# Modulation pieces of a two-layer diffusion trunk: placed in another order at the start, in attention and in the last norm gap, and a state term of the scan placed earlier

## What is computed

```python
sc, scc = jax.nn.silu(c), jax.nn.silu(c_ctx)
for l in range(DEPTH):
    m_lat = sc @ w_mod[l] + b_mod[l]          # 9 x 1024 values for the latent tokens
    m_ctx = scc @ w_mod[l] + b_mod[l]         # and for the context tokens
    h = half_ffn(h, shift0, scale0, gate0, ...)      # norm, modulate, SwiGLU, norm, gate
    u = modulate(h, g[2], shift1, scale1)
    y = token_mixing(u, ...)                  # MLA, windowed attention, gated DeltaNet, Mamba-2
    h = h + gate1 * rms_norm(y @ w_out, g[3])
    h = half_ffn(h, shift2, scale2, gate2, ...)

def modulate(x, g_pre, shift, scale):
    return rms_norm(x, g_pre) * (1.0 + scale) + shift
...
o = decay * (q @ S) + within-chunk part       # DeltaNet: S is the state, carried over 4 chunks
```

## Time and profile before

| | |
|---|---|
| median of 3 runs | 2270.41 us (2266.66 to 2270.74) |
| the profiled execution | 2268.9 us, its span 2267.0 us |
| mean granted TensorE clock | 0.961 of full |
| TensorE matmul busy | 2116.7 us, 93% |
| VectorE, ScalarE, GpSimd busy | 1088.5, 804.9, 213.8 us |
| read from HBM | 255.97 MB |

### The profile page before, as it was taken

The page is one execution under the profiler, slowest core; times in us unless marked ns, Lnnn a source line. Parts: engine busy times, 40 slices in busy tenths (PEclk is TensorE's granted clock), DMA queues, the critical chain, the costliest instruction groups (busy, mean ns, idle before and its releaser), DMA issues.

```text
span 2267.0 us, 31510 instructions
## 1 busy us (share of the span) xinstructions
PE 2116.7 (93%) x13261; PEld 1740.9 (77%) x13261; DVE 1088.5 (48%) x1598; ACT 804.9 (36%) x1277; POOL 213.8 (9%) x312
## 2 busy tenths in 40 slices
PE   6999999899989988999999899999989987888997
PEld 4778888687845876888888688888869765778997
DVE  4323233576284476433334633333464547576555
ACT  3322223354345433321232422122344434334443
POOL 0000000100013441000000200000020022420000
PEclk8999999999999999999999899999968999998999
DMA  9464352423235514323423342432332312434662
GB/s 286 129 194 114 118 131 77 151 75 98 67 102 186 186 57 130 93 70 107 112 76 101 112 112 64 121 104 70 108 121 65 119 38 94 131 103 121 177 169 83
DMA packets 403325, 259.07 MB, mean 114 GB/s; under 512 B 21850, under 2 KB 401904, under 8 KB 403184
## 3 DMA queue, kind: packets, MB, share of 16 engines
q1 hardware_dynamic: 403184, 257.06, 38.9%
HBM read 255.97 MB, written 1.05 MB: 113 GB/s over the span
## 4 chain that ended last, share of the span: by engine, by line
PE 81%; DVE 11%; ACT 4%; issue 2%; SPq 1%; DMA 0%; POOL 0%; POOLq 0%; DVEq 0%; ACTq 0%
PE bank L827 23%; PE bank L828 22%; PE bank L829 22%; PE bank L750 2%; PE bank L732 1%; DVE uT L2048 1%; DVE wl L1984 1%; PE bank L1174 1%; PE bank L1077 1%; ACT wh L1488 1%; DVE uT L2046 1%; PE bank L1106 1%; PE bank L779 1%; PE bank L771 1%; SPq L568 1%
## 5 line engine op out<-in xcount | busy, mean ns | idle before, releaser
L827 PE MATMUL bank<-uh,wh 128*128 128x512 f32 (+1 forms) x1504 | 549.6, 365 | 22.8 <-DVE ul L2054 15.5
L828 PE MATMUL bank<-ul,wh 128*128 128x512 f32 (+1 forms) x1504 | 546.3, 363 | 0.0
L829 PE MATMUL bank<-uh,wl 128*128 128x512 f32 (+1 forms) x1504 | 546.2, 363 | 0.0
L1984 DVE TENSOR_TENSOR wl<-ring,wh 128x2048 fp32r<-128x2048 f32 (+1 forms) x155 | 312.5, 2016 | 161.2 <-ACT wh L1488 160.4
L1488 ACT ACTIVATE wh<-ring 128x2048 fp32r<-128x2048 f32 (+1 forms) x158 | 267.2, 1691 | 302.9 <-PE bank L829 293.5
L827 PEld LDWEIGHTS bank<-uh,wh 128*128 128x128 f32 x1504 | 286.7, 191 | 72.0 <-issue 17.2
L829 PEld LDWEIGHTS bank<-uh,wl 128*128 128x128 f32 x1504 | 286.4, 190 | 43.8
L828 PEld LDWEIGHTS bank<-ul,wh 128*128 128x128 f32 x1504 | 286.8, 191 | 42.7
L827 PE MATMUL bank<-hh,wh 128*128 128x512 f32 (+1 forms) x704 | 255.5, 363 | 1.4 <-DVE wl L1984 1.4
L828 PE MATMUL bank<-hl,wh 128*128 128x512 f32 (+1 forms) x704 | 255.2, 363 | 0.0
L829 PE MATMUL bank<-hh,wl 128*128 128x512 f32 (+1 forms) x704 | 255.2, 362 | 0.0
(11 more groups left out here) (321 smaller groups left out, 2772.4 us busy)
## 6 DMA issues: line engine op xcount, KB each, us to landing
ring<-in_ffn_w_dram SPq DMA_DIRECT2D x176, 512.0 KB, 5.2
ring<-in_w_mod_dram SPq DMA_DIRECT2D x136, 512.0 KB, 4.6
ring<-in_ffn_w_dram SPq DMA_DIRECT2D x64, 384.0 KB, 3.6
...
```

Source lines behind the costliest of these rows:

```text
L827: pe.matmul(bank, w_hi, x_hi, start=first, stop=False)
L828: pe.matmul(bank, w_hi, x_lo, start=False, stop=False)
L829: return pe.matmul(bank, w_lo, x_hi, start=False, stop=last)
L1984: TT(low[:, b, 0:floats], at, high[:, b, 0:floats].bitcast(F32), ALU.subtract).then_inc(wl_ready, 1)
```

## The change

At the start, two modulation pieces are loaded ahead of the first weight piece and six behind it; the eight are taken in pairs of one shift and one scale piece (`START_COLUMN`), each pair gives the gains of two feature blocks (`start_gains`), and the last two pairs are multiplied between the products of the first weight piece (`first_piece`). In attention the turn of a modulation row stands behind the scores of the next pair, and the column copy behind that pair's second exponential. Three pieces of layer 1's attention are moved to its middle gap. In the last scan step `add_state` stands ahead of `split_out`.

```diff
--- before.py
+++ after.py
@@ -118,13 +118,13 @@
-    MOD_PLAN = {("start", 0): RING, ("spare", 0): 4, ("ffn0", 0): 9, ("ffn1", 0): 3, ("gap0", 0): 3, ("mix", 0): 27, ("gap1", 0): 3,
-                ("gap2", 0): 3, ("gap0", 1): 3, ("mix", 1): 13}
+    MOD_PLAN = {("start", 0): 2, ("start1", 0): 1, ("spare", 0): 5, ("ffn0", 0): 9, ("ffn1", 0): 3, ("gap0", 0): 3, ("mix", 0): 27, ("gap1", 0): 3,
+                ("gap2", 0): 3, ("gap0", 1): 3, ("mix", 1): 10, ("gap1", 1): 3}
     assert sum(MOD_PLAN.values()) == LAYERS * MOD_PIECES
     MOD_AFTER = {("up0", 0, 0): ("ffn0", 0), ("up1", 0, 0): ("ffn1", 0)}
-    GAP_BEFORE = {("in", 0): ("gap0", 0), ("up0", 0, 1): ("gap1", 0), ("up0", 1, 0): ("gap2", 0),
-                  ("in", 1): ("gap0", 1)}
+    GAP_BEFORE = {("up0", 0, 0): ("start1", 0), ("in", 0): ("gap0", 0), ("up0", 0, 1): ("gap1", 0), ("up0", 1, 0): ("gap2", 0),
+                  ("in", 1): ("gap0", 1), ("up0", 1, 1): ("gap1", 1)}
     for l in range(LAYERS):
@@ -319,11 +319,17 @@
         crow = view(29696, P)
-        spare = view(8192, 4, 2048)
+        spare = [view(at, 2048) for at in (20480, 22528, 24576, 10240, 14336)]
         uTf = uT[:, :, :].rearrange("p k t -> p (k t)")
         HEAD_DMAS, MOD_PARAM_DMAS, PARAM_DMAS = 4, LAYERS * 2, 2 + LAYERS * 15
-        START_MODS = MOD_PLAN["start", 0] + MOD_PLAN["spare", 0]
+        START_COLUMN = (0, 4, 1, 5, 2, 6, 3, 7)
+        def column_of(g):
+            l, p = divmod(g, MOD_PIECES)
+            return l, START_COLUMN[g] if g < KC else p
         NORM_AT = (195, 195, 193, 194)
@@ -505,7 +511,7 @@
-        MIX_PIECES = ((15, 8, 4, 0), (5, 4, 4, 0))
+        MIX_PIECES = ((15, 8, 4, 0), (2, 4, 4, 0))
@@ -571,7 +577,7 @@
             def mod_piece(g):
-                l, p = divmod(g, MOD_PIECES)
+                l, p = column_of(g)
                 n = MOD_PIECE[g]
@@ -595,6 +601,14 @@
                 return srcs
+            def spare_mods():
+                for i in range(MOD_PLAN["spare", 0]):
+                    l, p = column_of(MOD_FIRST["spare", 0] + i)
+                    src = rows(w_mod[l])[:, :, p * 256:(p + 1) * 256]
+                    dst = spare[i].rearrange("p (k w) -> p k w", k=KC)
+                    for h in (0, 4):
+                        sp.dma_start(dst[:, h:h + 4, :], src[:, h:h + 4, :]).then_inc(sem(f"spare_landed{i}"), 16)
@@ -603,6 +617,8 @@
                             mod_pieces(GAP_BEFORE.get((f"up{part}", l, f)))
+                        if (l, f, part, j) == (0, 0, 0, 0):
+                            spare_mods()
                         if ffn_mod(l, f, part, j) is not None:
@@ -624,13 +640,6 @@
                     sp.dma_start(dst, src).then_inc(sem("mod_params_in"), 16)
-            for i in range(MOD_PLAN["spare", 0]):
-                g = MOD_FIRST["spare", 0] + i
-                src = rows(w_mod[0])[:, :, g * 256:(g + 1) * 256]
-                dst = spare[:, i, :].rearrange("p (k w) -> p k w", k=KC)
-                for h in (0, 4):
-                    sp.dma_start(dst[:, h:h + 4, :], src[:, h:h + 4, :]).then_inc(sem(f"spare_landed{i}"), 16)
             def params(i):
@@ -739,7 +748,7 @@
                     pe.wait_ge(sem(f"spare_landed{i}"), 32)
-                    weights = spare[:, i, :]
+                    weights = spare[i]
                 else:
@@ -828,6 +837,23 @@
+            def first_piece():
+                def blocks(first, last):
+                    for k in range(first, last):
+                        wait_low(pe, 0, 0, k)
+                        for g in range(2):
+                            ws = slice((g * KC + k) * P, (g * KC + k + 1) * P)
+                            done = split_product(ps[g][:, :], (wh[:, 0, ws], wl[:, 0, ws]), (uh[:, k, :], ul[:, k, :]),
+                                                 k == 0, k == KC - 1)
+                            if k == KC - 1:
+                                done.then_inc((w1_done, pieces_done)[g], 1)
+                mod_work(4, 6, banks=(6, 7))
+                blocks(0, 2)
+                mod_work(6, 8, banks=(6, 7))
+                blocks(2, 8)
             def ffn(l, f, hs):
@@ -840,6 +866,9 @@
                         pe.wait_ge(gated, g0 + j - 1 + GATE_CREDIT)
+                        if (l, f, part, j) == (0, 0, 0, 0):
+                            first_piece()
+                            continue
                         fresh = part == 0 and j == 0
@@ -1114,13 +1143,13 @@
                 for p in range(pairs + 2):
-                    if p and att_mod(l, p - 1) is not None:
-                        mod_turn(att_mod(l, p - 1), ps[7])
                     if p < pairs:
                         biases(2 * p + 1)
+                    if p and att_mod(l, p - 1) is not None:
+                        mod_turn(att_mod(l, p - 1), ps[7])
                     if p >= 2:
@@ -1409,14 +1438,13 @@
             pe.wait_ge(cond_ready, 1)
-            mod_work(0, 4, banks=(0, 1))
+            mod_work(0, 2, banks=(0, 1))
             start_sums()
             setup_params(0, ps[2])
-            mod_work(4, 6, banks=(0, 1))
             spread(0, ps[PRE_BANK], (0, 1))
-            mod_work(6, START_MODS, banks=(0, 1))
-            pe.wait_ge(mod_copied, START_MODS)
+            mod_work(2, 4, banks=(6, 7))
+            pe.wait_ge(mod_copied, 4)
             for l in range(LAYERS):
@@ -1542,6 +1570,8 @@
                 for m in range(KC):
+                    if p == 0 and m in (2, 6):
+                        mod_work(*{2: (4, 6), 6: (6, 8)}[m], banks=(6, 7))
                     if 0 in hs:
@@ -1761,10 +1791,10 @@
                         exp(2 * p)
+                    if p < pairs:
+                        exp(2 * p + 1)
                     if p and att_mod(l, p - 1) is not None:
                         mod_column_out(att_mod(l, p - 1), ps[7])
-                    if p < pairs:
-                        exp(2 * p + 1)
                     if p:
@@ -1923,12 +1953,11 @@
             load_sqrt()
-            mod_work(0, 4, banks=(0, 1))
+            mod_work(0, 2, banks=(0, 1))
+            round_piece(PIECES["up0", 0, 0][0], 2048)
+            norm(0, ps[PRE_BANK], (0, 1))
             setup_mod_params()
-            norm(0, ps[PRE_BANK], (0, 1))
-            mod_work(4, 6, banks=(0, 1))
-            mod_work(6, START_MODS, banks=(0, 1))
-            round_piece(PIECES["up0", 0, 0][0], 2048)
+            mod_work(2, 4, banks=(6, 7))
             prenorm_blocks(0, 0)
@@ -2010,6 +2039,18 @@
+            def start_gains(i):
+                dve.wait_ge(mod_copied, 2 * i + 2)
+                at = slice(2 * i, 2 * i + 2)
+                both = modT[:, 0, 0:2 * KC, :].rearrange("p (s m) v -> p s m v", s=2)[:, :, at, :]
+                bias = prm[:, 0, 0:2 * KC].rearrange("p (s m) -> p s m", s=2)[:, :, at]
+                link(TT(both, both, wide(bias, 2), ALU.add))
+                link(STT(gpre[:, 0, at], modT[:, 0, KC + 2 * i:KC + 2 * i + 2, :], 1.0,
+                         wide(prm[:, 0, 72 + 2 * i:74 + 2 * i], 2), ALU.add, ALU.mult))
+                if i == 0:
+                    V.memset(small[:, 58:59], 0.0).then_inc(mod_ready, 1)
             def post_gains(l, j):
@@ -2043,6 +2084,8 @@
                             wait_x(dve, p - 1, m)
+                        elif m % 2 == 0:
+                            start_gains(m // 2)
                         TT(u[:, m, t0:T], xT[:, m, t0:T], ps[PRE_BANK][:, t0:T], ALU.mult).then_inc(x_scaled, 1)
@@ -2497,12 +2540,14 @@
                             finish_inverses(l, 0).then_inc(sem("first_inverses"), 1)
+                        add_state(n, ts, [gate(2, d, 0) for d in range(2)])
                         if early_out(l):
                     if outputs:
-                        add_state(n, ts, [gate(2, d, 0) for d in range(2)])
+                        if n < NT - 1:
+                            add_state(n, ts, [gate(2, d, 0) for d in range(2)])
                         dve.wait_ge(sem("og_ready"), f + 1)
@@ -2619,9 +2664,8 @@
             norm(0, (0, 1))
+            split_rest(PIECES["up0", 0, 0][0], 2048)
             dve.wait_ge(sem("params_act"), 1)
-            pre_gains(0, 0)
-            split_rest(PIECES["up0", 0, 0][0], 2048)
             prenorm_blocks(0, 0)
```

## The result

The changed kernel takes 2257.52 us in the median of five runs (2256.56 to 2260.51). The ratio to the kernel before is 0.995, with a 95% interval of 0.9935 to 0.9964: 8 to 15 us less. Run again beside others it took 2258.02 us, ratio 0.9946 (0.9928 to 0.9965). The forecast was 2256.5. The profiled execution is the slowest of its five, 2260.51 us, so that its span is only 8.3 us under the one of the earlier trace rows.

A forecast was written before the change was run, and what follows sets the result against it. TensorE was taken as the bound (81% of the chain, VectorE 11%), with gains only where it waits. Terms -7.0 - 6.2 - 0.3 - 1.8 + 2.2 = -13.1 gave 2256.5 us, range 2248 to 2263.

The forecast's parts named there:

- The start, -7.0: Start: with loads reordered, the second weight piece begins at 53.4 to 55.0, not 61.34; 7.0 us gained, ends 2.3 and 9.8.
- Ready at 53.2: Start: the second weight piece's low part, 8.0 us from the scaling of block 6 at about 45.2, is ready at 53.2.
- Layer 0's attention, -6.2: Layer 0's attention: 15 waits for a modulation row, 8.5 us, mostly vanish; 6.2 us gained, ends 8.5 and 2.0.
- nothing is lost there, little is left to lose: Layer 0's attention: column copy behind the second exponential comes 2.6 us later, as TensorE reaches the product; no loss.
- the lower end: Layer 0's attention: gain of only 2.0 us if release by the second exponential takes back 0.3 a pair.
- the slower rival: Attention: the second exponential releases every product, each pair loses 0.9 us; +6.8, about 2276 us; chance 0.05.
- Layer 1's attention, -0.3: Layer 1's attention: time freed by three fewer pieces lies ahead of a wait that stays; 0.3 us gained, ends 0 and 3.6.
- the rival's 3.6: Layer 1's attention: the whole 3.6 us from the removed pieces comes through; -16.4 in all, about 2253 us; chance 0.10.
- The scan's end, -1.8: Scan's end, both layers: `add_state` moves into VectorE's idle; layer 1 gains 1.1, layer 0 0.7; ends 0.7 and 2.3.
- The middle gap, +2.2: Layer 1's middle gap: three more modulation pieces cost 2.2 us; ends 0.9 and 3.6.
- the dearer case: Layer 1's middle gap: without a raised clock the second piece costs 1.71 to 2.1 plus 0.95, near 3 us.
- the cheaper end: Layer 1's middle gap: the product raises the clock, the 20 sums behind it save 1.4 us, net cost 0.9.

## Why the prediction was right, and where it was wrong

**The start, -7.0.** Measured 6.5 in the trace and 6.4 in the kernel with the start alone. Two of its steps erred, in opposite directions. The third pair's columns came at 37.97, not at 35.7: its second piece landed 0.7 late, and the product and two turns ran at the low clock (1.94 and 1.0 each), where I had taken the chain at the full clock. These 2.3 us were handed on through the 12 products, so that the last pair's columns came at 46.74, not 44.6. Then the 36 products ran at the full clock from their start and took 8.0 us, less than the 8.8 to 10.4 of the sum. "Ready at 53.2" was 54.73. Of the 6.5 us 4.4 hang on the interleaving, as the kernel with the last pair ahead shows.

**Layer 0's attention, -6.2.** Measured 6.04 in the windows and 6.1 alone. But the step "nothing is lost there, little is left to lose" failed. It was taken from one pair in which the maximum came early, the tenth; the same pair waited 0.84 us in the changed kernel. In seven pairs the copy behind the second exponential held the product, 5.1 us in all. TensorE's idle time fell by only 2.5 (87.34 - 77.76 to 81.30 - 74.19); the other 3.6 is busy time, which shrank as the clock of the stage rose from 0.98 to 1.00 (each trace with the old turn has 0.96 or 0.98 here, each with the new 1.00). How much of the 3.6 that accounts for I can't divide. That the size was right is luck, by two errors: the second exponential's price was not near nothing but 3.75 us, and the gain without it is 9.8, above the upper end of 8.5. The price is 0.25 us a pair, near the 0.3 that the lower end had allowed and under the 0.46 from which the slower rival would have been true: its mechanism was there, at about half that size.

**Layer 1's attention, -0.3.** Right. To the second level step, the one that the forecast went by, it is 60.28 us against 60.67, 0.4 less. To the first step it takes 56.9 to 57.6 us with two pieces or five, old turn or new, in all ten other kernels with so many; both traces of the kernel before have 58.5, at a clock of 0.91. Of the rival's 3.6 nearly all was waited away ahead of the levels.

**The scan's end, -1.8.** Mis-sized: 1.99 + 1.20 = 3.2 in the traces. Layer 1 was right (1.1 forecast, 1.2). In layer 0 the step that erred is the price of working beside GpSimd, which I had scaled by a third. The rows show an addition of about 1 us, whatever the length: the pair of adds took 1.97, not 0.76; the split 3.25 (before 3.12), not 2.29; the pair of adds in `last_y` 2.70, not 1.76; its last operation before 1.65, not 0.69. The scaling at L2629, which has one of its two inputs in PSUM, took 0.72 beside GpSimd and 0.74 without it. So the move itself gave nothing there. But it delayed `last_y`'s last operation until GpSimd had ended, and that fell from 1.65 to 0.69: VectorE's chain from L2507 to its last scale is 17.05 us against 18.02. The other half of the gain, 1.0, lies behind this chain: the transposes and what follows them took 4.95 us at a clock of 1.00, not 5.98 at 0.75. All nine traces with the new order have 22.1 us here and transposes of 1.97, all five with the old have 24.0 to 24.3 and 3.4 to 3.7, so this clock goes with the change. That GpSimd's work makes the difference is read from rows that coincide; no run had its work taken away.

**The middle gap, +2.2.** In the windows 16.97 against 14.98 in the kernel without the pieces, 2.0, and 3.0 against the kernel before, whose gap had more clock (0.71 against 0.52). From the first sum to the spread it is 8.61 against 5.57 to 5.86, so 2.8 to 3.0, near the dearer case. The product did not raise the clock at once, as the cheaper end assumed; the stretch ahead of these sums, with the first piece in it, is 0.5 to 0.8 shorter. The kernel with this part alone lost 3.6 (0.9 to 6.1). Behind the gap the low clock of its trace is a further 1.4 to 2 us that the forecast has no term for, if it belongs to the change.

The terms as measured, -6.5 - 6.0 + 0 - 3.2 + 2.0 to 3.0, give -12.7 to -13.7; forecast was -13.1. The medians give 11 to 13. That the two single traces differ by 8.3 alone is for the larger part the clock in stages that nothing changed: 3.1 us ahead of layer 0's attention and 3.2 in levels and scan are not there in other traces of the same code. So the mechanisms of the start and of layer 1's attention held; attention's and the scan's terms came out by errors in opposite directions or by a part that the sum lacked, and that the whole is within 1 us of the forecast is in part luck.
